# Gate weights behind the last gathered rows, q's norm in the exponent's scale, and a new order of buffers and splits

## The reference

```python
z = rms_norm(h, mix_norm_gain) @ w_in                   # 2048 -> 2112
y_pool = pool_mixer(z[..., :1024], w_pool, pool_scale)
y_mla = mla(...)    # q = rms_norm(rms_norm(c_q) @ w_uq), k likewise, rope on 64 of 192, 8 heads
h = h + concat(y_pool, y_mla) @ w_out
h = h + peer(rms_norm(h, ffn_gain), ...)
h = h + sigmoid(rms_norm(h, ple_gain) @ w_ple_gate) * (p @ w_ple_proj)
...
# peer: 8 heads x 16 experts for each token
act = gelu(einsum('tkd,td->tk', expert_u[ib], xb))
return einsum('tk,tkd->td', act * gb, expert_v[ib])
```

## Time and profile before

| | us |
|---|---|
| median of 3 runs | 2455.74 (2451.46 to 2457.87) |
| profiled execution, its time | 2456.61 |
| profiled execution, its span | 2455.2 |
| busy: TensorE, VectorE, GpSimd, ScalarE | 2123.2, 1407.9, 670.5, 649.0 |
| gathers (queue of GpSimd) | 536.90 MB of 751.23 MB moved |

### The profile page before, as it was taken

One profiled execution on the slowest core, in us unless ns is written; L12 is line 12 of the kernel. 1 busy time (PEld: TensorE's weight loads), 2 busy tenths in 40 slices (PEclk: granted clock), 3 DMA queues, 4 the chain that ended last, 5 costly groups with the idle time before them and its releaser, 6 DMA issues.

```text
span 2455.2 us, 19571 instructions
## 1 busy us (share of the span) xinstructions
PE 2123.2 (86%) x7564; PEld 1357.0 (55%) x7564; DVE 1407.9 (57%) x1842; ACT 649.0 (26%) x922; POOL 670.5 (27%) x523
## 2 busy tenths in 40 slices
...
GB/s 273 163 154 89 185 298 408 413 422 421 422 421 421 421 422 418 422 422 421 421 422 422 421 421 422 421 399 124 177 212 193 166 169 172 155 205 190 190 180 143
DMA packets 105356, 751.23 MB, mean 306 GB/s; under 512 B 11952, under 2 KB 11952, under 8 KB 14384
## 3 DMA queue, kind: packets, MB, share of 16 engines
q0 software_dynamic: 73728, 536.90, 52.7%
q1 hardware_dynamic: 29376, 207.63, 23.6%
...
## 4 chain that ended last, share of the span: by engine, by line
PE 53%; DMA 35%; DVE 6%; issue 2%; POOL 2%; ACT 1%; ACTq 0%; SPq 0%; DVEq 0%; POOLq 0%
PE ps L354 37%; DMA W<-in_expert_v,idx 24%; PE ps L741 12%; DMA raw<-in_expert_v,idx 4%; DMA raw<-in_expert_u,idx 2%; DMA W<-in_expert_u,idx 2%; DMA xT_rows<-in_expert_u,idx 1%; DMA wlo_row<-in_expert_v,idx 1%; DVE wlo L1371 1%; PE ps L375 1%; POOL W L307 1%; DVE W L1753 1%; DVE xT_rows L1753 1%; ACT whi L919 1%; DMA whi_row<-in_expert_u,idx 1%
## 5 line engine op out<-in xcount | busy, mean ns | idle before, releaser
L354 PE MATMUL ps<-whi,xT 128*128 128x512 f32 x2544 | 615.9, 395 | 12.0 <-ACT whi L919 10.6
L741 PE MATMUL ps<-W 128*128 128x512 f32 x1024 | 477.5, 610 | 147.6 <-DMA W<-in_expert_v,idx 120.6
L1371 DVE TENSOR_TENSOR wlo<-raw,whi 128x2048 fp32r<-128x2048 f32 x195 | 445.5, 2288 | 274.0 <-ACT whi L919 273.8
L354 PEld LDWEIGHTS ps<-whi,xT 128*128 128x128 f32 x2544 | 480.3, 190 | 116.0 <-issue 6.5
L919 ACT ACTIVATE whi<-raw 128x2048 fp32r<-128x2048 f32 x195 | 372.3, 1914 | 469.5 <-PE ps L354 270.0
L1753 DVE CUSTOM_DVE_ANT_0 W<-W 128x2048 f32<-128x2048 f32 x128 | 293.3, 2291 | 295.1 <-DMA W<-in_expert_u,idx 294.9
L741 PEld LDWEIGHTS ps<-W 128*128 128x128 f32 x1024 | 188.2, 192 | 426.8 <-issue 384.9
L354 PE MATMUL ps<-wlo,xT 128*128 128x512 f32 x1272 | 316.5, 391 | 9.3 <-DVE wlo L1371 9.3
L741 PE MATMUL ps<-raw,W 128*128 128x512 f32 x536 | 252.2, 614 | 65.4 <-DMA raw<-in_expert_v,idx 62.9
L354 PEld LDWEIGHTS ps<-wlo,xT 128*128 128x128 f32 x1272 | 239.5, 189 | 60.6 <-DVE wlo L1371 10.9
L307 POOL DMA_INDIRECT W<-in_expert_v,idx x132 | 189.3, 1434 | 276.8 <-PE ps L741 262.4
...
## 6 DMA issues: line engine op xcount, KB each, us to landing
raw<-in_weights SPq DMA_DIRECT2D x196, 1024.0 KB, 4.9
...
W<-in_expert_u,idx POOLq DMA_INDIRECT x128, 16.5
...
W<-in_pool_op ACTq DMA_DIRECT2D x1, 1024.0 KB, 5.1
```

Source lines behind the costliest of these rows:

```text
L354: return pe.matmul(ps[:, (banks_of(b) if bank is None else bank) + t, 0:cols_n], x[:, q0 + qn * 4 + k, s], w_[:, cs], start=start, stop=stop)
L741: m = pe.matmul(ps[:, (4 if t == 0 else 0) + b, :], diag[:, i % DIAGS, :], slots[SLOT_OF[n]][:, b * NC:(b + 1) * NC], start=(i % ROWS_OF_T ...
L1371: v.tensor_tensor(lo, raw[:, RAW_OF[c], :], hi.bitcast(F32), ALU.subtract).then_inc(sem["lo_done"], 1)
```

## The change

- x's parts 1, 2 and 3 are loaded one by one behind chunks 0, 1 and 2, chunk 0 straight after part 0. ScalarE and VectorE split chunk c + 1 ahead of x's part c + 1, and TensorE turns x's next part inside a chunk's hi matmuls.
- Chunk 18 is split by ScalarE before the latent turn, by VectorE behind all eight blocks of pool output.
- q is not multiplied by its root. Its 1/sqrt(sum + 192 eps) becomes the scale operand of the exponent and of the maximum. q's rotation takes the gain in a small table (`rope_w`) and is done between UKV's chunks; q is turned after the first W_out chunk, k after the fourth. The squares' junk output goes to SBUF.
- Chunk 46 goes to raw 2, and 47 and on swap raw 0 and 1. The first lap has five homes (0, 1, 8, 9, 3) for rows 0 to 4, then six; home 2 waits for chunk 46's lo.
- From row 280 on the homes are 2, 3, 10, 11, 12, 13, 0, 1 to the end, eight also for the last rows.
- SyncE waits for the landing of row 510 (`NEAR_END`) before it issues chunk 60. Chunks 60 and 61 are split and multiplied after the rows, for both tiles.

```diff
 TAIL = PICKS - LAG
 ROW_ORDER = [("u", i) for i in range(LAG)] + [(kind, i + d) for i in range(PICKS) for kind, d in (("u", LAG), ("v", 0)) if i + d < PICKS]
 ROW_AT = {what: n for n, what in enumerate(ROW_ORDER)}
+FIRST_LAP = 5
 FEW_ROWS = ROW_AT["u", 72]
 LATE_ROWS = ROW_AT["u", 144]
-LAST_ROWS = 16
+NEAR_END = len(ROW_ORDER) - 2
 QUERY_AT = {6: 3, 7: 6, 8: 18, 9: 22, 10: 26, 11: 30, 12: 41, 13: 46, 14: 51, 15: 56}
 TURN_AT = {1: 9, 2: 34, 3: 60}
...
 def slot_of_row(n):
-    last = n - (len(ROW_ORDER) - LAST_ROWS)
+    if n < FIRST_LAP:
+        return (0, 1, 8, 9, 3)[n]
     if n < FEW_ROWS:
-        return (0, 1, 2, 3, 8, 9)[n % 6]
-    if last >= 0:
-        return (10, 11, 12, 13, 0, 1)[last % 6]
+        return (0, 1, 2, 8, 9, 3)[(n - FIRST_LAP) % 6]
     if n >= LATE_ROWS:
-        return (10, 11, 12, 13, 0, 1, 2, 3)[(n - LATE_ROWS) % 8]
+        return (2, 3, 10, 11, 12, 13, 0, 1)[(n - len(ROW_ORDER)) % GR]
     return (n - FEW_ROWS + 4) % GR
...
 TWO_RAW = range(C_PQ + 4, C_GATE + 2)
 ONE_SPLIT = range(C_PQ + 4, C_PROJ)
-RAW_OF = [c % 2 if c in TWO_RAW else c % RAW for c in range(CHUNKS)]
+RAW_OF = [2 if c == TWO_RAW.start else (c + 1) % 2 if c in TWO_RAW else c % RAW for c in range(CHUNKS)]
 RAW_ROUND = [RAW_OF[:c + 1].count(RAW_OF[c]) for c in range(CHUNKS)]
...
+        head_junk = W[:, 15488:15488 + NH * QH]
+        rope_w = tmp[:, 768:1024].rearrange("p (k t f) -> p k t f", k=4, t=NT)
...
             load_x(0)
-            load_x(1)
             for c in range(CHUNKS):
-                if c == 1:
-                    load_x(2)
-                    load_x(3)
+                if c in (1, 2, 3):
+                    load_x(c)
                 if RAW_BEFORE[c] is not None:
                     sp.wait_ge(sem["lo_done"], RAW_BEFORE[c] + 1)
+                if c == C_GATE:
+                    row_landed(sp, NEAR_END)
                 if c == TWO_RAW.stop:
...
             for n, (kind, i) in enumerate(ROW_ORDER):
                 if ROW_BEFORE[n] is not None:
                     rows_used(g, ROW_BEFORE[n])
-                if n == 4:
+                if n == 2:
                     g.wait_ge(sem["used"], C_PQ + 3)
+                if n == FIRST_LAP + 2:
+                    g.wait_ge(sem["lo_done"], C_PQ + 5)
                 if n == FEW_ROWS:
...
                 for k in range(nk):
+                    if k == 2 and between:
+                        between()
...
-            pe.wait_ge(sem["load_x0"], 32)
-            entry(E_MIX, 0)
-            pe.wait_ge(sem["load_x1"], 32)
-            entry(E_MIX, 1)
-            block_step(B_IN, 0, 0, 4)
...
+            def first_entry(part):
+                pe.wait_ge(sem[f"load_x{part}"], 32)
+                entry(E_MIX, part)
+
+            first_entry(0)
+            for qn in range(4):
+                entry_ready(E_MIX, qn)
+                block_step(B_IN, qn, qn, 4, between=(lambda: first_entry(qn + 1)) if qn < 3 else None)
 
...
+            pool_step(0)
+            for g in range(4):
+                part_turn(g, q_of, g)
+            pool_step(1)
+            pe.wait_ge(sem["heads_ok"], 2)
+            for g in range(2):
+                part_turn(4 + g, lambda t, k: qrh[:, t, k * 128:(k + 1) * 128], g)
+            pool_step(2)
+            pool_step(3)
+            pe.wait_ge(sem["k_ok"], 2)
+            for g in range(4):
+                part_turn(6 + g, k_of, g)
+            for g in range(2):
+                part_turn(10 + g, lambda t, k: krh[:, t, k * 128:(k + 1) * 128], g)
             pe.wait_ge(sem["head_put_v"], 6)
...
-                if i in (200, 202, 204, 206, 208, 210):
-                    gate_part((i - 200) // 6, 0, (i - 200) // 2 % 3)
...
+            for part in range(3):
+                gate_part(0, part)
+            gate_part(1, 0)
+            gate_part(1, 1).then_inc(sem["hi_used"], 1)
+            gate_turn(1, 2)
+            gate_part(1, 2).then_inc(sem["used"], 1)
+            gate_turn(1, 3)
...
             entry(E_MIX, 0, 0)
             split(0)
+            split(1)
             entry(E_MIX, 1, 0)
-            split(1)
+            split(2)
             entry(E_MIX, 2, 0)
-            split(2)
+            split(3)
             entry(E_MIX, 3, 0)
+            split(4)
             square_rows(E_MIX, 0)
...
-            pool_out(range(4))
-            split(18)
-            pool_out(range(4, 8))
+            pool_out(range(8))
...
+            for c in range(19, 23):
+                split(c)
+            a.wait_ge(sem["pool_mm"], 8)
+            for e in (evac_of(B_UQ + 2), evac_of(B_UQ + 1)):
+                a.wait_ge(*e)
             for t in range(NT):
                 if t:
-                    a.wait_ge(sem["head_sq"], 2)
-                else:
-                    for e in (evac_of(B_UQ + 2), evac_of(B_UQ + 1)):
-                        a.wait_ge(*e)
-                ss = st[:, 16 + 16 * t:24 + 16 * t]
-                squares(heads(q[:, t, :], NH), QH, ss).then_inc(sem["head_sq"], 1)
-                root(2 * t + 1, ss, "head_mean", "head_root")
-                split(26 + 2 * t)
+                    a.wait_ge(sem["q_sq"], 1)
+                squares(heads(q[:, t, :], NH), QH, st[:, 16 + 16 * t:24 + 16 * t]).then_inc(sem["q_sq"], 1)
+                split(23 + t)
+            split(25)
+            split(26)
+            a.wait_ge(sem["q_sq"], 2)
+            def put(dst, g, gain, n, i):
+                a.wait_ge(sem["head_T"], n)
+                scale = 1.0 if gain is None else colv[:, gain:gain + 1]
+                a.activation(dst[:, g * 512:(g + 1) * 512], ps[:, 4 + i % 4, :], ACT.Copy, scale=scale).then_inc(sem["head_put_a"], 1)
+
+            a.wait_ge(sem["used"], C_OUT)
+            for e in (evac_of(B_UKV + 3), evac_of(B_UKV + 2)):
+                a.wait_ge(*e)
+            for t in range(NT):
+                ss = st[:, 24 + 16 * t:32 + 16 * t]
+                if t:
+                    put(qT, 1, COLS["q_nope"], 2, 1)
+                    put(qT, 3, COLS["q_nope"], 4, 3)
+                    a.wait_ge(sem["head_sq"], 1)
+                squares(heads(kv[:, t, :], NH), QN, ss)
+                a.activation(head_junk[:, 1024:1024 + QR], z[:, t, D:Z_W], ACT.Square, accum_out=st[:, 10 + t:11 + t]).then_inc(sem["head_sq"], 1)
+                root(t + 1, ss, "head_mean", "head_root")
                 if t == 0:
-                    for e in (evac_of(B_UKV + 3), evac_of(B_UKV + 2)):
-                        a.wait_ge(*e)
-                ss = st[:, 24 + 16 * t:32 + 16 * t]
-                a.wait_ge(sem["head_sq"], 2 * t + 1)
-                squares(heads(kv[:, t, :], NH), QN, ss)
-                a.activation(junk[:, 1024:1024 + QR], z[:, t, D:Z_W], ACT.Square, accum_out=st[:, 10 + t:11 + t]).then_inc(sem["head_sq"], 1)
-                root(2 * t + 2, ss, "head_mean", "head_root")
-                split(27 + 2 * t)
-
-            puts = ([(qT, g, COLS["q_nope"]) for g in (1, 3)] + [(kT, g, COLS["k_nope"]) for g in (1, 3)] + [(qrT, 1, None), (krT, 1, None)])
-            a.wait_ge(sem["used"], C_OUT)
-            for (dst, g, gain), n in zip(puts, (2, 4, 6, 8, 10, 12)):
-                a.wait_ge(sem["head_T"], n)
-                s = 1.0 if gain is None else colv[:, gain:gain + 1]
-                a.activation(dst[:, g * 512:(g + 1) * 512], ps[:, 4 + g % 4, :], ACT.Copy, scale=s).then_inc(sem["head_put_a"], 1)
+                    root(1, st[:, 16:40].rearrange("p (t n) -> p t n", n=8)[:, 0:3:2, :], "q_mean", "q_root")
+                split(27 + t)
+
+            put(qrT, 1, None, 6, 5)
+            split(29)
+            put(kT, 1, COLS["k_nope"], 8, 7)
+            put(kT, 3, COLS["k_nope"], 10, 9)
+            put(krT, 1, None, 12, 11)
...
+            exps(0, prob[0], st[:, 16:24], st[:, 40:48], st[:, 48:56], 1, "score_max", "score_exp")
...
-                if i in (104, 110):
-                    split(60 + (i - 104) // 6)
-
-            for part in range(4):
-                gate_entry(1, part)
+
+            split(C_GATE)
+            gate_entry(1, 0)
+            gate_entry(1, 1)
+            split(C_GATE + 1)
+            gate_entry(1, 2)
+            gate_entry(1, 3)
...
+            def q_rotate(t, part):
+                half = QR // 2
+                qt = heads(q[:, t, :], NH)[:, :, QN:QH]
+                x1, x2 = (qt[:, :, 0:half], qt[:, :, half:QR]) if part == 0 else (qt[:, :, half:QR], qt[:, :, 0:half])
+                a_, b_ = heads(rot_a, NH), heads(rot_b, NH)
+                settled()
+                if t and not part:
+                    v.wait_ge(sem["heads_ok"], 1)
+                own(v.tensor_tensor(a_, x1, per_dim(rope_w[:, 2 * part, t, :], NH, half), ALU.mult))
+                own(v.tensor_tensor(b_, x2, per_dim(rope_w[:, 2 * part + 1, t, :], NH, half), ALU.mult))
+                settled()
+                m = v.tensor_tensor(heads(qrh[:, t, :], NH)[:, :, part * half:(part + 1) * half], a_, b_, ALU.add if part else ALU.subtract)
+                if part:
```

(78 more changed lines are left out.)

111 lines of the change are left out of this document (28 added, 83 removed).

## The result

The changed kernel takes 2433.9 us (median of 4 runs, 2429.4 to 2435.4) against 2455.9 us before: ratio 0.991, 95% interval 0.9896 to 0.9923. The same file run five more times on another occasion gave 2431.35 us (2429.7 to 2436.8), ratio 0.9905 (0.9888 to 0.9922). The prediction was 2431.5 us, range 2423 to 2444. The profiled execution took 2434.62 us with a span of 2433.2.

A forecast was written before the change was run, and what follows sets the result against it. DMA bytes at 421 GB/s were taken to bound the gather stage, TensorE the rest. Seven terms summed to -24.4 us from the profiled 2456.61, giving 2432.2, or 2431.3 from the median; stated 2431.5, range 2423 to 2444.

The forecast's parts named there:

- Part 1: Start: loading x's part 1 behind chunk 0 and splitting chunk 3 early saves 1.1 us (0 to 1.9).
- Part 2: Pool output before chunk 18's split: shorter TensorE wait and full clock at chunk 18, -3.9 us.
- Part 3: Head norms, chunk 25 to first score matmul: fewer TensorE waits for VectorE's q and k norms, -9.2 us.
- Part 4: Before the gathers: chunk 46 loads in idle DMA time and dot 5's wait goes, -1.5 us (0 to -2.5).
- Part 5: Gather stage: chunks 60 and 61 leave its middle, -5.0 us; chunks 62 to 65 leave its end, -9.6.
- Part 6: Row 280: new order of the last homes makes rows wait while the queue drains, +5.0 us (3 to 15).
- Part 7: Last dot to gate product: late rows faster, then chunks 60 and 61 follow, +0.9 us in all (-0.5 to +5).
- A: Row 280: ring refills as slowly as in a full queue, row 281 15.5 us late; 2442 us, chance 0.10.
- C: Row 280: ring needs two 16.5 us trips in series, kernel slower; 2459.5 us, chance 0.02.
- B: Head norms or chunk 18: k norms late or half clock stays, about 6 us lost; 2437.5, chance 0.12.
- E: After the rows: chunks 60 to 63 land one by one behind TensorE, 6 us more; 2437.5, chance 0.08.
- D: Gather stage: homes set the pace, so removing loads returns nothing, 14.6 us lost; 2446, chance 0.05.

The follow-up runs named there:

- experiment 5: Kernel before the change, with only pool output ahead of chunk 18's split and the new head norms and turns added; 2443.02 us, ratio 0.995.
- experiment 7: Changed kernel with twelve extra 128x256 multiplications, some 5 us, on VectorE ahead of the last operation of k's norm; 2435.77 us.
- experiment 6: Changed kernel with chunk 46 back in raw 0 and the first lap back to six homes; 2432.07 us.
- experiment 1: Changed kernel run again with no edit; 2431.35 us.
- experiment 4: Kernel before the change, with one wait added: SyncE issues chunk 62 only when row 510 has landed; 2444.62 us, ratio 0.9952.
- experiment 2: Changed kernel with slots 2 and 3 moved one place forward per lap in the last homes' order from row 280; 2425.04 us, ratio 0.9874.
- experiment 3: Changed kernel with k's six turns ahead of chunk 28 instead of behind it; 2429.38 us.
- experiment 8: Changed kernel with both the step-by-step order of the last homes and k's turns ahead of chunk 28; 2424.65 us, ratio 0.9879.

## Why the prediction was right

The time was right within the noise, and the three large parts (3, 5 and 6) were right in size and cause. That the sum came within 0.5 us of the trace at chunk 63 (-24.4 and -24.85) is partly luck: up to dot 80 the gain was 1.5 less than in the sum and part 6 cost 0.7 more, while 1.1 between dots 160 and 252, in no term, and 1.6 in part 7 went the other way.

- **Part 1**, -1.1: measured -1.96 at chunk 4. Half clock ended within the first chunk: eight matmuls took 3.75 and eight transposes 1.39, the next eight matmuls 2.11. It lies just beyond the end of the range. The cause is read from one trace; no run has this part alone.
- **Part 2**, -3.9: -3.7 (chunk 19 -5.69, less 1.96). The gap is 1.08 (1.2 worked out) and the clock stays; experiment 5 shows the same gap and 3.88 for the 16 matmuls.
- **Part 3**, -9.2: -9.3 from chunk 25 to the first score product. The step "if VectorE took 6 us more it would cost nothing" failed (experiment 7); the real margin was 2.0 us, at chunk 28's split in the same queue. It did not matter, as VectorE was on time. The sign that the prediction names, a first score product at 189.5, does not follow from its own sum: 165.9 less the 1.1 of part 1 plus 28.7 is 193.5, and 192.76 was measured. The squares in SBUF take 0.35 where those into PSUM took 0.31, yet start 0.35 apart in both:

```profile
149.77 0.35 ACT L1027 ACTIVATE W<-W 128x192 f32<-128x192 f32 x1
150.11 0.35 ACT L1027 ACTIVATE W<-W 128x192 f32<-128x192 f32 x1
```
and before the change:
```profile
181.81 0.31 ACT L1019 ACTIVATE ps<-W 128x192 f32<-128x192 f32 x1
...
182.15 0.31 ACT L1019 ACTIVATE ps<-W 128x192 f32<-128x192 f32 x1
```

- **Part 4**, -1.5: nothing measurable (experiment 6). The step that failed is "there the gain is what the chain of dots gains. Dot 5 now waits 1.55": that wait goes, and VectorE waits 1.81 for ScalarE ahead of dot 6 instead (in experiment 1). Chunk 46 did move ahead: SyncE issues a load at 293.26, before the first gather (311.74), where experiment 6 issues none between 290 and 300. Up to dot 80 executions with this part end anywhere from -14.1 to -16.6 against before.
- **Part 5**, -5.0 and -9.6: -5.00 from dot 80 to dot 96, which experiment 5, with the chunks left in the middle, does not have; -9.6 from dot 252 to 255, and experiment 4 shows this second one by itself, 10.0. Another 0.9 comes at dots 200 to 208, where TensorE no longer has the gate products of the first tile between rows. That is not its cause: experiments 2, 3 and 8 lack these products too and win 0.1 at most there. The cause of the 0.9 stays open.
- **Part 6**, +5.0: +5.1 at dot 145, +5.7 by dot 160, and experiment 2 takes it away. The gather that finds an empty queue, issued at 1052.21, is read at 1057.76: 5.55 us, the 5.5 of the sum. By the Trainium skill, "DMA: Bandwidth & Descriptors", section "Bandwidth", a 1 MB transfer takes 6.15 us by itself; here issue and all took less, in the one gather that the trace shows by itself, so the row's bound was the better guide. The last row before it had landed by 1052.20, when TensorE began on it.
- **Part 7**, +0.9: from the last dot to chunk 62 39.65 before and 40.55 now, +0.90. But the sum should have gone to chunk 63: before, chunk 62 waited 2.19 and ran at half clock; now it follows chunk 61 without a wait at full clock. There it is -0.7. Inside the term two errors cancelled. Chunk 60 was issued at 1632.88 as worked out, but ScalarE waited for it until 1638.93, 6.05 us instead of 4.9, and its hi was there 3.5 after the last row's matmuls, not 2.3; TensorE waited 1.60 for it. The first eight matmuls then ran at full clock, 2.1 us in all, where the sum had 0.4 each, 3.2. And the working's own 24.8 against 25.4 is -0.6, not -0.8; measured were 24.4, -1.0.
- **Not in the sum**: half clock, 4.3 us in the scores, of which about half was taken up by dot 80, and 2.85 behind chunk 63, which stayed. The sum of -24.4 against -22.0 in this execution is that 2.85 and little else; the second execution had -25.2.

Of the rivals, A and C fell with the trace, since the ring healed in one short trip; B and E with it too (chunk 18 at full clock, 16.1 us to chunk 62, though chunk 60 alone came 1.2 late); D with experiment 4. What stays open is why about half of a delay ahead of the gathers is made good by dot 80 in the changed kernel's first execution and in experiment 7, while the 13.3 us won in experiment 5 arrive in full. Six homes, the query projections on TensorE and the clock act together there, and no run separates them.
